# Sums of q's squares made at the start of VectorE's slot, ahead of the weight split and the norm portion

## What is computed

```
def cross_attention(h, m, w_q, w_kv, w_o, q_norm, k_norm):
    q = rms_norm((h @ w_q).astype(f32).reshape(bsz, L, X_HEADS, X_DH), q_norm) * (X_DH ** -0.5)
    kv = (m @ w_kv).astype(f32).reshape(bsz, m.shape[1], 2, X_HEADS, X_DH)
    k = rms_norm(kv[:, :, 0], k_norm)
    v = kv[:, :, 1]
    p = jax.nn.softmax(jnp.einsum('bqhd,bmhd->bhqm', q, k), axis=-1)
    o = jnp.einsum('bhqm,bmhd->bqhd', p, v).reshape(bsz, L, D_MODEL)
    return o.astype(h.dtype) @ w_o
```

## Time and profile before

| | |
|---|---|
| median of 3 timed runs | 2537.8 us (2537.19 to 2540.1) |
| the profiled execution's own time | 2539.81 us |
| its span, first to last instruction | 2538.0 us |
| busy: PE, DVE, ACT | 2443.0 us (96%), 1531.7 us (60%), 1150.5 us (45%) |
| chain that ended last, share by engine | PE 81%, DVE 12%, ACT 4%, issue 2%, DMA 1% |
| mean granted clock of TensorE | 0.986 |

### The profile page before, as it was taken

One profiled execution on the slowest core, in us unless ns is written; L12 is line 12 of the kernel. 1 busy time (PEld: TensorE's weight loads), 2 busy tenths in 40 slices (PEclk: granted clock), 3 DMA queues, 4 the chain that ended last, 5 costly groups with the idle time before them and its releaser, 6 DMA issues.

```text
span 2538.0 us, 35247 instructions
## 1 busy us (share of the span) xinstructions
PE 2443.0 (96%) x14102; PEld 2075.0 (82%) x14102; DVE 1531.7 (60%) x2599; ACT 1150.5 (45%) x2010; POOL 0.2 (0%) x4
## 2 busy tenths in 40 slices
PE   7997799899999999999999999999999999999999
PEld 4887576778888999899778888778788888888887
DVE  8988756767546755564565446656886645533332
ACT  4232336344433555544454444445665443423422
POOL 0000000000000000000000000000000000000000
PEclk9998899999999999999999999999999999999999
DMA  5324532255312455444224323223334423433332
GB/s 189 95 67 103 167 111 96 80 169 191 108 59 85 156 183 184 123 132 136 78 73 157 116 81 119 75 84 101 92 92 142 132 73 88 141 99 100 92 100 91
DMA packets 109667, 289.24 MB, mean 114 GB/s; under 512 B 18913, under 2 KB 41569, under 8 KB 108225
## 3 DMA queue, kind: packets, MB, share of 16 engines
q1 hardware_dynamic: 101392, 261.36, 33.5%
q10 hardware_dynamic: 8112, 25.63, 3.1%
HBM read 265.35 MB, written 19.50 MB: 112 GB/s over the span
## 4 chain that ended last, share of the span: by engine, by line
PE 81%; DVE 12%; ACT 4%; issue 2%; DMA 1%; SPq 0%; ACTq 0%; DVEq 0%
PE ps L1414 65%; PE ps L1504 2%; PE ps L338 2%; PE ps L1479 2%; PE ps L334 2%; DVE wlo L1391 1%; PE ps L1522 1%; PE ps L1546 1%; DVE ps L1697 1%; DVE ps L1696 1%; DVE yP L1698 1%; ACT yP L1565 1%; DMA wraw<-wt 1%; DVE x L555 1%; PE ps L1446 1%
## 5 line engine op out<-in xcount | busy, mean ns | idle before, releaser
L1414 PE MATMUL ps<-in_hP,whi 128*128 128x512 f32 x1336 | 541.1, 405 | 1.6 <-issue 1.6
L1386 ACT ACTIVATE whi<-wraw 128x1024 fp32r<-128x1024 f32 x430 | 452.2, 1053 | 194.1 <-PE ps L1414 128.7
L1391 DVE TENSOR_TENSOR wlo<-wraw,whi 128x1024 fp32r<-128x1024 f32 x431 | 523.4, 1218 | 22.7 <-ACT whi L1386 22.4
L1414 PE MATMUL ps<-in_hP,wlo 128*128 128x512 f32 x1336 | 522.9, 391 | 0.0
L1414 PE MATMUL ps<-in_lP,whi 128*128 128x512 f32 x1336 | 522.1, 391 | 0.0
L1414 PE MATMUL ps<-in_hS,whi 128*128 128x256 f32 x1088 | 320.0, 294 | 5.6 <-DVE x L1719 4.3
L1414 PE MATMUL ps<-in_lS,whi 128*128 128x256 f32 x1088 | 309.4, 284 | 0.0
L1414 PE MATMUL ps<-in_hS,wlo 128*128 128x256 f32 x1088 | 309.3, 284 | 0.0
L1414 PEld LDWEIGHTS ps<-in_hP,whi 128*128 128x128 f32 x1336 | 252.4, 189 | 63.1 <-issue 11.0
L1414 PEld LDWEIGHTS ps<-in_lP,whi 128*128 128x128 f32 x1336 | 252.3, 189 | 55.5 <-issue 5.0
L1414 PEld LDWEIGHTS ps<-in_hP,wlo 128*128 128x128 f32 x1336 | 251.9, 189 | 54.2
(11 more groups left out here) (471 smaller groups left out, 3685.7 us busy)
## 6 DMA issues: line engine op xcount, KB each, us to landing
wraw<-wt SPq DMA_DIRECT2D x432, 512.0 KB, 3.5
wraw<-wt ACTq DMA_DIRECT2D x17, 512.0 KB, 4.1
k_scratch<-region_P SPq DMA_DIRECT2D x16, 256.0 KB, 3.1
v_scratch<-vtmp SPq DMA_DIRECT2D x32, 128.0 KB, 3.0
x<-x_in SPq DMA_DIRECT2D x4, 768.0 KB, 6.8
mix_u<-x SPq DMA_DIRECT2D x32, 64.0 KB, 3.4
mix_mem<-mem_in ACTq DMA_DIRECT2D x4, 512.0 KB, 6.5
x<-x_in ACTq DMA_DIRECT2D x1, 2048.0 KB, 12.7
```

What stands on the lines that cost most here:

```text
L1386: nc.scalar.activation(whi[:, (n + 3) % NHI, :, :], wraw[:, ws(n), :, :], ACT.Copy).then_inc(wh.sem, 1)
L1391: nc.vector.tensor_tensor(wlo[:, ws(n), :, :], wraw[:, ws(n), :, :], whi[:, (n + 3) % NHI, :, :].bitcast(F32), ALU.subtract).then_inc(wr.s ...
L1414: last = nc.tensor.matmul(ps[:, m % 2, 0:N[prod.g]], w_[:, k, :], x_[:, k, :], start=(k == 0 and j == 0), stop=(k == KT - 1 and j == 2))
```

## The change

In a slot whose `before` is a tile of a q product, DVE now does `dve_post` of that tile first: ahead of `low`, of the norm or cross-attention steps, and of the slot's own tile. In all other slots it stays behind them. For an even tile `dve_post` does nothing, so 16 additions are moved, one per head and product. The other engines' instructions keep their order.

```
                         for step in steps:
                             if step[0] == "gla" and step[2] in (2, 5):
                                 dve_gla(v, *step[1:])
+                        early = before is not None and before[0].kind == "q"
+                        if early:
+                            dve_post(v, before)
                         if t is not None and t[2] + NHI - 2 < NT:
                             low(v, t[2] + NHI - 2)
                         for step in steps:
...
                         for step in steps:
                             if step[0] == "gla":
                                 dve_gla_post(v, *step[1:])
-                        if before is not None:
+                        if before is not None and not early:
                             dve_post(v, before)
                         before = t
```

## The result

The changed kernel takes 2523.7 us in the median of 4 runs (2523.0 to 2525.7), the kernel before 2538.3 (2537.2 to 2540.1) beside it: ratio 0.9946, interval 0.9933 to 0.9959, so 14 us or 0.5% faster. The forecast was 2523.4. The page's first part shows the same work in a shorter span; 5.4 us of PE's busy time are gone too, though no matmul was taken away.

The account below looks back on a forecast made before the run. PE, busy 96% of the span, was taken as the bound. 6.4 + 2.85 + 1.12 + 4.05 = 14.4 us won: 2525.4 from the profiled 2539.8, 2523.4 from the median 2537.8; own range 2520 to 2527, whole range 2519.5 to 2531.

Parts of the forecast that it names:

- The five places: Where PE waits for the sum: heads 0 and 2 of q0/S, head 3 of q0/P, q1/S, q1/P; 10.3 us together.
- Place one: Head 0 of q0/S, wait 3.25 us: the sum starts 1.74 us earlier, 1.5 us of wait stay.
- The clock behind place one: After head 0 of q0/S: if the clock stays up, PE needs 6.2 us instead of 9.20, 3.0 won.
- my sign that no granted clock of 0.50 would stand near 655: Expected trace evidence behind head 0 of q0/S: no granted clock of 0.50 there, nor near 742 or 2060.
- the first rival: Low clock stays behind places one, three and five, losing 1.4, 1.7 and 1.7 us: gain 9.5, time 2528.3; chance 0.17.
- Place two: Head 2 of q0/S, wait 2.51 us: small matmuls start near 664.1 instead of 670.99, 0.5 us of wait left.
- My chain: Timing followed through q0/S to head 2's small matmuls: 6.9 us won; 6.4 taken, being 0.5 early for the kernel before.
- Places three and five: Head 3 of q0/P and q1/P: waits of 1.11 and 2.33 go whole; with the clock 2.85 and 4.05 us won.
- Place four: Head 3 of q1/S: its wait goes whole, 1.12 us won.
- What is added: DVE instructions behind the sum also wait for the square; split 2.1 us later at head 0 of q1/S; cost taken nothing.
- the split's 3.9 us of reserve: At head 0 of q1/S: 0.6 + 0.4 + 2.9 us before PE needs the split, hiding its delay.
- The second and third rivals: Second: DVE's backlog stays the bound of q0/S, 2529.2, chance 0.07; third: the sum waited for its square, 2534.8, 0.06.

Follow-up runs that it names:

- the two parts that hold the five: Two kernels moving fewer sums than the change: those of q0/S only, 0.9973 of the kernel before; those of head 3 of q0/P, q1/S, q1/P only, 0.9966.
- The filled waits: Changed kernel with 3 calls of matmuls on constants in PE's remaining wait at place one: 0.9936 of the kernel before, 2522.5 us.
- one experiment: Only the four sums of q0/S moved, against the kernel before: 0.9973, 2530.8 us.
- the three with the wait filled: Matmuls on constants put into PE's waits: kernel before, overfilled 0.9992; kernel before, right number 0.9981; changed kernel 0.9936; all against the kernel before.
- the two where only 0.88 us of wait were left: Changed kernel, in q0/S ACT's square first and the sum in its own slot behind the split, run twice: 0.9926 and 0.9932 of the kernel before.
- the first four experiments: Against the kernel before: q0/S sums only 0.9973; head 3 of the other three only 0.9966; 11 unwaited sums only 1.0002; PE's waits overfilled, nothing moved, 0.9992.
- the two kernels with filled waits: Kernel before with matmuls on constants in PE's three long waits, no sum moved: too many 0.9992, 2536.2 us; right number 0.9981, 2533.9 us.

## Why the prediction was right, point by point

- The five places were the right ones, and the only ones: the 11 other sums, moved alone, give nothing, and the two parts that hold the five give the whole gain. Shown.
- Place one: the sum's 1.74 us reach PE whole (1.74), and 1.5 us of wait stay (1.51). Shown by the trace.
- The clock behind place one: the term of 3.0 us was too large. The change gave 1.44, for a low stretch remained, and so my sign that no granted clock of 0.50 would stand near 655 failed. That was the first rival's mechanism at one of its three places: it had priced a loss of 1.4 there, and 1.6 came. What the prediction says came before the fall, the wait and then the one-column matmuls, doesn't hold at place one, where the clock was low before they started. The filled waits show that with PE at work in the 1.5 us the rest comes too (29.9 against 31.4 us).
- Place two: I took 0.5 us of remaining wait, from DVE's 12.97 busy microseconds. Measured 0.16. q0/S gave 5.5. My chain had said 6.9: the low stretch took 1.6 of it, place two gave 0.1 more. With the clock kept, in the changed kernel with its wait filled, PE needs 12.9 us from place one to place two, as in the chain (651.2 to 664.1), and the stage gains 7.0. So the chain was right, and the 0.5 that I had taken off for the forecast of 6.4 was not needed. Head 2's matmuls came at 665.73 and not near 664.1, by the low stretch.
- Places three and five: 3.07 and 4.26 against 2.85 and 4.05. The stretch from small matmuls to next tile is 4.55 us at both, where 4.6 had been taken from clean slots. The wait and the clock went together, as forecast. Yet the clock's 1.7 us at place three are not tied to the wait alone: in one experiment they went with the wait still there. 0.16 of each difference is the overlap of matmuls that the idle time leaves out.
- Place four: 1.28 against 1.12, the same 0.16.
- What is added: 2.0 us later splits (2.1 forecast) and no wait. The reserve is real, as the 11 sums show. One slot earlier the sum costs 13 us against the kernel before, but mostly by the probabilities; that the split's 3.9 us of reserve are what hides the delay was argued from the row and not tested apart.
- The sum: 14.1 by place, and 14.4 with the 0.3 between places four and five, against a forecast of 14.4. q0/S came 0.9 short; the head-3 places gave 0.6 more and the 0.3 belong to no term. So the closeness of 2523.7 to 2523.4 is in part luck; single runs of either kernel differ by more.
- The second and third rivals are excluded by the trace: DVE's idle time in the stage did shrink (12.88 us busy of 14.28 from head 0's sum at 650.89 to head 2's at 665.17, where it had been 12.97 of 17.46), and in the kernel before DVE was not idle for the square ahead of any of the five sums that PE waited for.

## What to carry to other kernels

Read a wait of the matrix engine together with the granted clock behind it: here waits of 10.3 us, of which 1.7 are left, stood for a gain of 14. An instruction whose result the matrix engine needs at the end of a slot belongs at the start of that slot on the engine that makes it, ahead of work that has a slot in reserve; but not a slot earlier, where it has to wait for its own input and holds up the rest (13 us lost here), unless that input is made early too, as in q0/S with ACT's square first (2.3 us of the stage won). And before an operation is moved up on one engine, look at what it passes in every slot, the first one too, and at who waits for that.

## What the runs showed of the hardware

- Low clock came after PE had stood still, and stayed away when the same time was filled with matmuls that nobody reads: at place one 0.50 in all eight traces with a wait of 1.11 to 3.25 us, 1.00 in the three with the wait filled, and 1.00 in the two where only 0.88 us of wait were left.
- But a wait does not decide it by itself. The wait of 1.11 us at place three was followed by a clock of 0.50 in the kernel before and by 1.00 in the kernel with q0/S moved; the wait of 2.5 us at place two by 1.00 in the kernel before and by 0.68 in the mean of three microseconds with the filled waits. At place three nothing that runs just before differs, only when the place came; the same holds at place two for the two kernels with filled waits: from place one on both run at the full clock and take nearly the same time to place two (15.05 and 15.17 us), both have a wait of 2.50 us there, and it was followed by 1.00 in the one and by the low clock in the other. The Trainium skill says that the moment at which the clock is decided is free-running and "doesn't reset when your kernel starts" (TensorE: Matmul & The Clock Gate, Part 1). Place three agrees with that, by 0.50 and 1.00 behind the same wait of 1.11 us.
- This also spreads the timed runs. Beside the first four experiments 25 runs of the kernel before lay between 2531.8 and 2540.3 us. The kernel with the 11 sums comes to place one at 648.98 instead of 652.93, 4 us earlier, and what lies ahead of that place is the same in both; the mean granted clock up to the norm's matmul is 0.97 in the one and 0.96 in the other. So below some 4 us a stage's length read in the trace tells more than the total.
